# Memory cross-attention stage of a hybrid decoder step: how the eight new queries reach all 128 partitions

## The reference

```python
def mem_attention(q, mk, mv):
    s = jnp.einsum('bthd,bmhd->bhtm', q.astype(jnp.float32), mk.astype(jnp.float32)) * MEM_DIM ** -0.5
    p = jax.nn.softmax(s, axis=-1)
    return jnp.einsum('bhtm,bmhd->bthd', p, mv.astype(jnp.float32)).astype(q.dtype)
```

## Time and profile before

| | |
|---|---|
| Median of 3 runs | 1361.85 us (1358.86 to 1362.75) |
| Profiled execution | 1357.2 us |
| Its span | 1355.5 us |
| Granted TensorE clock, mean | 0.955 |
| TensorE busy | 1228.2 us (91%) |
| VectorE busy | 831.7 us (61%) |
| DMA, mean | 174 GB/s |

### The profile page before, as it was taken

One profiled execution on the slowest core, in us unless ns is written; L12 is line 12 of the kernel. 1 busy time (PEld: TensorE's weight loads), 2 busy tenths in 40 slices (PEclk: granted clock), 3 DMA queues, 4 the chain that ended last, 5 costly groups with the idle time before them and its releaser, 6 DMA issues. The chain is left out here.

```text
span 1355.5 us, 22629 instructions
## 1 busy us (share of the span) xinstructions
PE 1228.2 (91%) x7621; PEld 1030.1 (76%) x7621; DVE 831.7 (61%) x1096; ACT 470.8 (35%) x873; POOL 388.6 (29%) x261
## 2 busy tenths in 40 slices
PE   5885999999999858999999995899999998999998
PEld 5884777768767538998998984688888876568886
DVE  5747899998994543979696982344533344524221
ACT  6513555545546741132322313222222131422211
POOL 2466544443530015656556650000000000000000
PEclk9997899999999889999999997999999998999999
DMA  8765686586582447466566541856566653645220
GB/s 284 227 210 158 197 251 216 164 251 212 174 268 87 134 88 229 143 196 199 166 186 216 183 127 38 256 171 195 177 181 203 190 173 128 201 153 166 68 63 31
DMA packets 201029, 235.80 MB, mean 174 GB/s; under 512 B 13763, under 2 KB 122514, under 8 KB 200906
## 3 DMA queue, kind: packets, MB, share of 16 engines
q1 hardware_dynamic: 195282, 218.18, 52.3%
q0 software_dynamic: 5632, 16.18, 3.3%
HBM read 213.78 MB, written 20.63 MB: 173 GB/s over the span
## 5 line engine op out<-in xcount | busy, mean ns | idle before, releaser
L134 PE MATMUL bank<-xh,w_hi 128*128 128x344 f32 x864 | 290.2, 336 | 15.5 <-DVE bank L2230 15.5
L134 PE MATMUL bank<-xh,w_lo 128*128 128x344 f32 x864 | 279.3, 323 | 0.0
L134 PE MATMUL bank<-xl,w_hi 128*128 128x344 f32 x864 | 279.2, 323 | 0.0
L2126 POOL TENSOR_TENSOR ring<-ring,cp_q 128x1024 f32<-128x1024 f32 x64 | 165.5, 2605 | 128.4 <-DMA ring<-cache_sb_k 128.0
L2126 POOL TENSOR_TENSOR bp_keys<-bp_keys,bp_q 128x1024 f32<-128x1024 f32 x64 | 169.9, 2676 | 110.6 <-DMA bp_keys<-cache_sb_k 110.4
L134 PEld LDWEIGHTS bank<-xh,w_hi 128*128 128x128 f32 x864 | 165.9, 192 | 45.2 <-issue 16.3
L134 PEld LDWEIGHTS bank<-xl,w_hi 128*128 128x128 f32 x864 | 165.7, 192 | 1.7 <-issue 1.5
L134 PEld LDWEIGHTS bank<-xh,w_lo 128*128 128x128 f32 x864 | 165.4, 191 | 0.0
L381 PE MATMUL bank<-xh,w_hi 128*128 128x344 f32 x408 | 137.6, 337 | 2.1 <-DVE w_lo L360 2.1
L381 PE MATMUL bank<-xl,w_hi 128*128 128x344 f32 x408 | 133.7, 328 | 0.0
L381 PE MATMUL bank<-xh,w_lo 128*128 128x344 f32 x408 | 133.4, 327 | 0.0
(11 more groups left out here) (368 smaller groups left out, 2044.1 us busy)
## 6 DMA issues: line engine op xcount, KB each, us to landing
ring<-cache_sb_k SPq DMA_DIRECT2D x128, 256.0 KB, 2.9
cp_values<-cache_sb_v SPq DMA_DIRECT2D x128, 256.0 KB, 3.1
bp_keys<-cache_sb_k SPq DMA_DIRECT2D x128, 256.0 KB, 3.1
dp_values<-cache_sb_v SPq DMA_DIRECT2D x128, 256.0 KB, 2.8
ring<-w_in SPq DMA_DIRECT2D x36, 512.0 KB, 5.8
o_raw<-w_out SPq DMA_DIRECT2D x8, 1024.0 KB, 5.1
c_w_raw<-w_in SPq DMA_DIRECT2D x15, 512.0 KB, 5.0
o_mix<-mix SPq DMA_DIRECT2D x7, 1024.0 KB, 6.6
```

The lines of the kernel that those rows point to most:

```text
L134: last = self.nc.tensor.matmul(self.bank(j, c), w[:, j % 2, k, :], x[:, k, c * CH:(c + 1) * CH], start=(k == 0 and n == 0), stop=(k == KT ...
L2126: self.nc.gpsimd.tensor_tensor(self.keys[:, s], self.keys[:, s], q, ALU.mult).then_inc(self.scaled.sem, 1)
```

## The change

The products with the identity on VectorE and the products with ones on TensorE go, with the semaphores `diag_ready` and `q_spread`. In their place GpSimd's queue stores the 8 query columns of `qT` (128 partitions x 8 numbers) to a scratch tensor in DRAM laid out as [token, number], waits for that store, and loads the 1024 numbers back, broadcast to all 128 partitions, into the room of `probT` that is now called `q_wide`. VectorE waits for that load (`q_in`) and reads `q_wide` where it read the banks B5 and B6. In the new lines GpSimd waits first for the query tile to be taken and, from head 1 on, for the last product of the head before, which reads `probT`.

```diff
+        self.d_q_dram = scratch("new_memory_q", [MLH, NB, P])
...
+    q_wide = probT[:].rearrange("p s m t -> p (s m t)").rearrange("p (b d) -> p b d", b=NB)
...
             for i in range(MLH):
+                flow.wait_taken(pool, tile(i, 0))
+                if i:
+                    pool.wait_ge(weighted.sem, weighted.at(i, 0))
+                pool.sem_inc(sending, 1)
+                pool.dma_start(k.d_q_dram[i].rearrange("b d -> d b"), qT[:, T:NT], allow_slow_non_contiguous=True).then_inc(q_out.sem, 16)
+                pool.wait_ge(q_out.sem, q_out.at(i, 1))
+                pool.dma_start(q_wide.rearrange("p b d -> p (b d)"), k.d_q_dram[i:i + 1].rearrange("o b d -> o (b d)")
+                               .to_broadcast([P, NB * P])).then_inc(q_in.sem, 16)
                 pool.wait_ge(u_rows.sem, u_rows.at(i, 1))
...
-                flow.wait_taken(dve, tile(i, 0))
-                for b in range(NB):
-                    last = nc.vector.tensor_scalar(q_diag[:, b, :], k.ident[:], qT[:, T + b:T + b + 1], None, ALU.mult)
-                last.then_inc(diag_ready.sem, 1)
                 maximum(0)
                 maximum(1)
                 flow.split_lo(dve, tile(i, 2))
 
                 dve.wait_ge(keys_in.sem, keys_in.at(i, 1))
-                dve.wait_ge(q_spread.sem, q_spread.at(i, 1))
+                dve.wait_ge(q_in.sem, q_in.at(i, 1))
                 for g in range(2):
-                    q = quad((B5, B6)[g]).rearrange("p b (o d) -> p b o d", o=1).to_broadcast([P, 4, MB, P])
+                    q = q_wide[:, 4 * g:4 * g + 4, :].rearrange("p b (o d) -> p b o d", o=1).to_broadcast([P, 4, MB, P])
...
-                pe.wait_ge(diag_ready.sem, diag_ready.at(i, 1))
-                for g in range(2):
-                    last = nc.tensor.matmul((B5, B6)[g][:, :], k.ones[:], q_diag[:, 4 * g:4 * g + 4, :]
-                                            .rearrange("p b d -> p (b d)"), start=True, stop=True)
-                last.then_inc(q_spread.sem, 1)
```

More of the change, by code:

```diff
@@ L1200, in memory_and_pooling @@
     top, total, inv = sb("top", [P, 2, UB]), sb("total", [P, 2, UB]), sb("inv", [P, 2, UB])
-    q_diag = probT[:].rearrange("p s m t -> p (s m t)").rearrange("p (b d) -> p b d", b=NB)
+    q_wide = probT[:].rearrange("p s m t -> p (s m t)").rearrange("p (b d) -> p b d", b=NB)
     cache = k.ring[:, 2:4].rearrange("p s e c -> p (s e c)").rearrange("p (b m d) -> p b m d", b=NB, m=MB)
@@ L1234, in memory_and_pooling @@
     weighted, y_taken = S("weighted", UNITS), S("y_taken", 2)
-    diag_ready, q_spread, product_ready, s_ready, s_turned = S("diag_ready", 1), S("q_spread", 1), S("product_ready", 2), S("s_ready", 1), S("s_turned", 1)
+    q_out, q_in, product_ready, s_ready, s_turned = S("q_out", 1, 16), S("q_in", 1, 16), S("product_ready", 2), S("s_ready", 1), S("s_turned", 1)
     new_step, new_exp, new_back, new_taken = S("new_step", 4), S("new_exp", 1), S("new_back", 1), S("new_taken", 1)
@@ L1372, in _ @@
             for s in (small_set, top_ready, neg_ready, inv_ready, prob_ready, turned_taken, y_taken,
-                      diag_ready, product_ready, s_ready, new_step, new_taken, new_gated, buf_taken, u_rows, doubled,
+                      product_ready, s_ready, new_step, new_taken, new_gated, buf_taken, u_rows, doubled,
                       pooled_ready, pool_mixed):
@@ L1507, in _ @@
         def _(pe):
-            for s in (scored, turned, weighted, q_spread, s_turned, new_back, new_weighted,
+            for s in (scored, turned, weighted, s_turned, new_back, new_weighted,
                       buf_turned, u_turned, pool_done):
```

## The result

| | before | changed |
|---|---|---|
| median of 6 runs each, us | 1361.82 (1358.86 to 1367.25) | 1394.09 (1388.55 to 1395.81) |
| profiled execution: time / span, us | 1357.2 / 1355.5 | 1394.8 / 1393.1 |

The ratio of the runs is 1.0248 (95% interval 1.0217 to 1.028); the two medians are 32.3 us apart, a ratio of 1.0237, which lies in that interval. The forecast of 1358.3 us and its range up to 1366.0 are both missed.

A forecast was written before the change was run, and what follows sets the result against it. TensorE was taken to bound heads 1 to 3, and transfers head 0. Terms of -5.4 us (heads 1 to 3) and +1.9 us (head 0) sum to -3.5 us, from the median 1361.85 to 1358.3 us; range 1355.0 to 1366.0.

The forecast's parts named there:

- X: Heads 1 to 3: landing time of the 4-byte query store, taken as 3.9 us, bounds 1.8 and 7.7.
- The nearest row: Store of `out_C_sample`, 128 partitions x 8 pieces of 512 bytes from GpSimd's queue, landing after 3.9 us.
- Its upper bound: For the 4-byte store's landing: the store of `ends` under full load, 7.7 us.
- Y: Landing time of the 512 KB broadcast query load: 4.0 us in heads 1 to 3, 6.2 in head 0.
- Rival D: The store of single 4-byte numbers, 512 bytes apart, is dear and makes the kernel slower: 1373.7 us, chance 0.13.
- X + Y = 14: Dear-store case: store and load landings total 14 us, pages land 3.3 us late per head in heads 1 to 3, 1373.7 us.
- Head 0: Bound by transfers: the saved 1.8 us gains nothing, the new load costs 0 to 1.9 us, 1.9 taken.
- The page products moved up: Heads 1 to 3: removing the products with ones starts page products 1.8 us earlier per head, 5.4 us together.
- the product from SBUF: VectorE's big product of 2.35 us: reading spread queries from SBUF in place of PSUM was taken as free.
- Whatever is taken from TensorE shortens the head: Heads 1 to 3: TensorE is busy 74.41 of 75.00 us, so removing its work gains 1.8 us per head.
- heads of about 73 in place of 75 us: Sign in the profile after that would show the forecast right: shorter heads 1 to 3.
- The forecast's own sum of -3.5 us: Whole kernel: -5.4 us in heads 1 to 3 plus 1.9 us in head 0, chance 0.45.

The follow-up runs named there:

- the turned layout: Changed kernel with the scratch as [number, token], each partition storing one 32-byte piece, VectorE reading it strided: 1361.95 us, ratio 1.0005 to the kernel before.
- its repeat: The turned layout, unchanged against its first execution, executed a second time: 1365.34 us in one execution.

## Why the prediction was wrong

**The step that failed** is X, the landing of the 4-byte store: taken as 3.9 us, bounded at 7.7, measured 10.9 to 11.3 (11.2 to 11.6 less the turnaround) and 12.1 in head 0. The nearest row was chosen by the number of pieces. The experiments show that number to be nearly beside the point: the same 1024 pieces take 3.6 to 3.9 us, turnaround included, once they lie 64 bytes apart. Its upper bound, a store under full load, was no bound either, since no row before shows 1024 pieces of 4 bytes. The rule of the Trainium skill (DMA: Bandwidth & Descriptors, rules for kernel authors), one descriptor per element for a strided last dimension, warned of the right line, but the stores at 32 and 64 bytes apart fall under it just as much and are cheap. The traces show the rule only on ScalarE's queue, which has 1040 packets while it stores the 1024 pieces; GpSimd's queue shows 32 packets for 1024 pieces and for 128 alike.

**Y** was taken as 4.0 and measured 6.6, 5.4 and 4.9 us in heads 1 to 3, inside its bounds; 6.2 was taken in head 0 and 7.0 measured.

**Rival D** named the dear store and had 0.13. It was right in its sign and its place, but not in its geometry: it describes the pieces as lying 512 bytes apart. That is the distance between two pieces of one partition. The next partition's piece lies 4 bytes further on, so the store as a whole fills 4 KB without a gap, and pieces spread out are the cheap case. D was priced only up to X + Y = 14, where head 1 has 17.5, and it let the pages decide at the end. The profile shows the first consumer, the transposes of `s_col`. By the prediction's own numbers a product 18.45 us behind the scores has `s_col` ready at 23.1, where TensorE stands at 17.2 - 1.8 = 15.4: a wait of 7.7 us, and 7.56 is measured. The 1.5 us of lower clock behind the wait were in no term of the prediction.

**Head 0** was taken at +1.9 us for the load's share of the DMA engines. That size fits as far as single executions tell: head 0 is 1.6 us longer with the load alone and 1.4 with the turned layout, but -0.1 in its repeat, 2.3 and 2.4 with pieces 32 and 64 bytes apart, and 0.9 shorter where its code was left as before. The store was charged there with its latency alone. What it does to the other transfers, 8.25 us by itself, was not thought of.

**What held.** The page products moved up by 1.7 us in head 1, heads 1 to 3 would be 1.72 us shorter (1.8 taken), which is the removal on TensorE alone and leaves nothing for VectorE's removed work, and the product from SBUF takes 2.36 us where it took 2.35 from PSUM.

**A second step would have failed behind the first.** "Whatever is taken from TensorE shortens the head" is true of the stretch up to L1595; that the tail stays as it is was not asked. The sign "heads of about 73 in place of 75 us" fails with it: with the turned layout head 1 and its tail take 74.7 us, before 74.8. With X cured, the 5 us of heads 1 to 3 went into the longer tails, head 0 and the stretch behind the last head: 1.0005 and 0.9992. The forecast's own sum of -3.5 us would be 0.9974, just outside the interval of the turned layout (from 0.9978) and inside that of the load without the store (from 0.9967).

**What stays open.** How the memory or the DMA engines handle small pieces that lie close together, whether it is their distance or the extent they cover that counts, and why other transfers slow down for it, no run shows; nor what sets the length of the tails.

## What to carry to other kernels

Price a transfer by how its pieces lie in DRAM and not by their number alone. Here it was enough to let each partition write one contiguous piece of 32 bytes and to turn the layout where it is read, on an engine with room. Before a small store is put into a busy stretch, look at which transfers are under way then and who is close to waiting for them. And a microsecond taken from TensorE can be lost again in the next stretch in which its clock falls; read the granted clock there, and the time behind it, before the gain is added up.

## What was not expected of the hardware

A store of 4 KB in pieces of 4 bytes, 4 bytes apart, takes 11 us, and with the store alone the DMA engines together move 67 GB/s in the 12 us of head 0 around it where they moved 284; a page load of 256 KB takes 11.9 in place of 3.0 us. The DMA share does not tell it apart: in that stretch the engines are busy to 0.70, and in head 1 of the changed kernel, while the store runs, to 0.23 at 32 GB/s (the kernel before moved 122 GB/s in these 11 us of head 1):

```profile
945.40:956.60 11.20, 11.20 (x72) 8.82 (x71) 2.82 (x5) 5.31 (x12) 0.91 (x1) 1.00 0.23 32
```

and the four page loads of that stretch land after 10.1 us without TensorE noticing, since they are wanted later. ScalarE's queue stored the same pieces in 9.5 to 10.2 us in heads 1 to 3, so the price is not GpSimd's. The clock's cost behind the one-column products is 0 to 3.4 us for the same instructions: the tails take 19.7, 21.4 or 23.0 us.
